# Branch B of a two-layer diffusion step: softmax sums from ScalarE's accumulator, and two passes with the values in place of three

## The reference, cut to what matters

```
s_band = einsum(qb, kband)            # |i - j| <= 128, else -1e30
s_ctx  = einsum(qb, k_ctx)            # 128 cached context keys
s_sink = broadcast(sink)              # one logit per head
p = softmax(concat([s_band, s_ctx, s_sink]))
o = einsum(p_band, vband) + einsum(p_ctx, v_ctx)      # the sink's p is dropped
```

## Time and profile before

| | |
|---|---|
| runs | 1607.69, 1608.44 (median), 1612.07 us |
| the profiled execution's own time | 1607.28 us, span 1605.5 us |
| TensorE (matmul) | 1458.1 us busy, 91% |
| VectorE | 833.1 us, 52% |
| GpSimd | 781.1 us, 49% |
| ScalarE | 550.6 us, 34% |
| mean granted TensorE clock | 0.968 |
| branch B attention | about 376 to 521 us (layer 0) and 1175 to 1320 us (layer 1) |

### The profile page before, as it was taken

The page is one execution under the profiler, slowest core; times in us unless marked ns, Lnnn a source line. Parts: engine busy times, 40 slices in busy tenths (PEclk is TensorE's granted clock), DMA queues, the critical chain, the costliest instruction groups (busy, mean ns, idle before and its releaser), DMA issues.

```text
span 1605.5 us, 21685 instructions
## 1 busy us (share of the span) xinstructions
PE 1458.1 (91%) x8776; PEld 1316.6 (82%) x8776; DVE 833.1 (52%) x1257; ACT 550.6 (34%) x821; POOL 781.1 (49%) x542
## 2 busy tenths in 40 slices
PE   4998998999998999899919999989999989998995
PEld 3798888899887888898718888887998879998984
DVE  4675677453788411103665676764438774011056
ACT  3233554234642211223122245542345432221221
POOL 1444675324675434645342456762246754464453
PEclk9999999999999999999969999999999999999998
DMA  7312000212010444253113220002121012214311
GB/s 306 131 53 70 27 27 16 87 59 66 27 41 27 146 145 169 79 183 120 40 31 114 70 67 26 27 28 80 55 66 35 32 56 102 79 66 171 107 64 66
DMA packets 36612, 126.90 MB, mean 79 GB/s; under 512 B 5024, under 2 KB 5664, under 8 KB 36512
## 3 DMA queue, kind: packets, MB, share of 16 engines
q1 hardware_dynamic: 29808, 108.54, 19.9%
q10 hardware_dynamic: 6704, 16.97, 2.9%
HBM read 119.73 MB, written 5.77 MB: 78 GB/s over the span
## 4 chain that ended last, share of the span: by engine, by line
PE 79%; DVE 10%; POOL 4%; issue 2%; ACT 2%; DMA 0%; POOLq 0%; DVEq 0%; ACTq 0%
PE ps L833 41%; PE ps L785 6%; PE ps L787 6%; PE ps L786 6%; PE ps L928 2%; PE ps L930 2%; PE ps L980 2%; PE ps L957 2%; PE ps L977 2%; DVE o_inv L1494 2%; PE ps L956 2%; PE ps L978 2%; POOL w_lo L1589 1%; PE ps L850 1%; DVE x L1546 1%
## 5 line engine op out<-in xcount | busy, mean ns | idle before, releaser
L1589 POOL TENSOR_TENSOR w_lo<-raw,w_hi 128x1024 fp32r<-128x1024 f32 x150 | 363.4, 2430 | 353.6 <-ACT w_hi L1026 353.2
L833 PE MATMUL ps<-h_hi,w_hi 128*128 128x320 f32 x1280 | 299.3, 315 | 13.6 <-DVE g_c L1506 6.4
L833 PE MATMUL ps<-h_lo,w_hi 128*128 128x320 f32 x1280 | 293.6, 311 | 0.0
L833 PE MATMUL ps<-h_hi,w_lo 128*128 128x320 f32 x1280 | 293.0, 310 | 0.0
L1609 POOL TENSOR_TENSOR p_lo<-p_f,p_hi 128x512 fp32r<-128x512 f32 x164 | 212.8, 1301 | 154.9 <-ACT p_hi L1137 154.7
L833 PEld LDWEIGHTS ps<-h_hi,w_hi 128*128 128x128 f32 x1280 | 218.2, 189 | 34.5 <-issue 8.7
L833 PEld LDWEIGHTS ps<-h_lo,w_hi 128*128 128x128 f32 x1280 | 217.1, 190 | 2.5
L833 PEld LDWEIGHTS ps<-h_hi,w_lo 128*128 128x128 f32 x1280 | 216.1, 189 | 2.4
L1026 ACT ACTIVATE w_hi<-raw 128x1024 fp32r<-128x1024 f32 x150 | 154.8, 1050 | 99.2 <-DMA raw<-in_weights 44.4
L1521 DVE TENSOR_TENSOR gy<-ps,sg 128x640 f32<-128x640 f32 x32 | 26.4, 824 | 255.7 <-PE ps L833 255.6
L1444 DVE TENSOR_REDUCE top<-ps 128x1 f32<-128x512 f32 (+1 forms) x128 | 83.5, 657 | 120.7 <-PE ps L935 87.0
(11 more groups left out here) (164 smaller groups left out, 2589.7 us busy)
## 6 DMA issues: line engine op xcount, KB each, us to landing
raw<-in_weights SPq DMA_DIRECT2D x190, 512.0 KB, 3.3
raw_more<-in_weights SPq DMA_DIRECT2D x10, 512.0 KB, 10.8
x<-in_x_sample ACTq DMA_DIRECT2D x6, 512.0 KB, 8.2
x_mid<-x ACTq DMA_DIRECT2D x5, 512.0 KB, 4.4
x<-x_mid ACTq DMA_DIRECT2D x5, 512.0 KB, 6.5
y_sample<-x SPq DMA_DIRECT2D x4, 512.0 KB, 2.7
pack<-in_pack ACTq DMA_DIRECT2D x2, 528.0 KB, 4.7
x<-in_x_sample SPq DMA_DIRECT2D x2, 512.0 KB, 5.0
```

The lines of the kernel that those rows point to most:

```text
L833: last = pe.matmul(ps[:, s + half, 0:HALF], w[:, u % RING, cols], acts[:, k, half * HALF:(half + 1) * HALF], start=k == 0 and part == 0, s ...
L1589: did(pool.tensor_tensor(w_lo[:, n % RING, :], raw_tile(r), w_hi[:, n % RING, :], ALU.subtract), w_ready)
```

## The change

In branch B alone:

- `S` no longer serves only the maximum. VectorE takes the maximum and makes minus max(top, sink) in one more small instruction (`neg_made`); then ScalarE takes the exponential of the same scores in place in PSUM, with that as its bias and with `accum_out` into `sums`. The bank is drained by ScalarE now. In tile 0 these are four exponentials of 128 columns.
- `dg`, the sink's step, its `p_hi`, `p_lo`, its two passes and the ones tile are gone: 30 steps per layer remain. 
- New, `su` on VectorE: sums + exp(sink - max), reciprocal, and a split in hi and lo, four instructions of 128x4. New, `it`: a transpose of the 128x8 on TensorE, and VectorE spreads it over `inv_m` (8 x 512). New, `iv`: one matmul of 512 columns with `first_rows` (ones in 8 rows), whose result ScalarE copies to `inv_b` (64x512).
- `PV` has two passes: the stationary tile is [v_lo, v_hi] by `p_hi`, then [v_hi, 0] (or [0, v_hi] for the other head) by `p_lo`. So O comes in two halves of the rows. `O` on VectorE is, for odd and even heads each, a copy of one half (64x256 from PSUM), the addition of the other and the multiplication by the inverse. The bank is drained after the second addition.
- Order: `tick()`, which puts out the `O`, `og`, `oh`, `ol`, `iv` events that are due, comes before `ST` in both branches. In branch B, `it` stands before the `ST` three steps after the group's first, and `S`, `row`, `es`, `su` come after the step's `PV`. The filler is spread over 30 steps instead of 40.
- Banks: in branch B, `row`, `it` and `iv` take banks 2 and 3 in turn with `ST`; `S` has 0 and 1 for itself.
- `zeros` (GpSimd, small memset) and `neg_sink`, `two_by_four`, `first_rows` (small constants) are new.

```diff
@@ attention()
         if br == "b":
             early[max(first[g] - row_ahead, -1)].append(("es", l, br, g))
+            early[first[g]].append(("su", l, br, g))
...
         if i == len(group_slots(br, g)) - 1:
-            later.append([1, ("O", l, br, g, 0)])
-            later.append([2, ("O", l, br, g, 1)])
+            if br == "a":
+                later.append([1, ("O", l, br, g, 0)])
+                later.append([2, ("O", l, br, g, 1)])
+            else:
+                later.append([1, ("iv", l, br, g)])
+                later.append([2, ("O", l, br, g, 1)])
...
+    def turn_inverse(n):
+        if br == "b" and n >= 0 and steps[n][1] == 0:
+            out.append(("it", l, br, steps[n][0]))
+
     for n, (g, i) in enumerate(steps):
-        if group_slots(br, g)[i] == SINK:
-            out.append(("dg", l, br, g))
+        tick()
+        turn_inverse(n - lag)
         out.append(("ST", l, br, g, i))
-        out.extend(early[n])
-        tick()
+        if br == "a":
+            out.extend(early[n])
         if n >= lag:
             product(n - lag)
+        if br == "b":
+            out.extend(early[n])
         fill()
     for n in range(len(steps) - lag, len(steps)):
         tick()
+        turn_inverse(n)
         product(n)
@@ bank_plan()
-        elif kind in ("S", "row"):
+        elif kind in ("S", "row") and e[2] == "a":
             take(e, 1, turn["S"] % 2)
             turn["S"] += 1
...
+        elif kind in ("row", "it", "iv", "ST"):
             take(e, 1, 2 + turn["ST"] % 2)
             turn["ST"] += 1
@@ TensorE
+                    elif kind == "it":
+                        s = begin(e)
+                        pe.wait_ge(inv_made, NO[e] + 1)
+                        did(pe.transpose(ps[0:2 * GRP, s, 0:P], inv_r[:, NO[e] % 3, :].bitcast(F32), ident), filled[s])
+                    elif kind == "iv":
+                        s = begin(e)
+                        wait_drained(pe, ("it",) + e[1:])
+                        did(pe.matmul(ps[:, s, :], first_rows[:, :], inv_m[:, :], start=True, stop=True), filled[s])
...
+                            both, high = v_pair(slot_key, kv)
+                            pe.matmul(ps[:, b, :], both, p_hi[:, n % 3, :], start=i == 0, stop=False)
                         pe.wait_ge(p_lo_made, n + 1)
                         last = pe.matmul(ps[:, b, :], high, p_lo[:, n % 3, :], start=False, stop=ends)
@@ ScalarE
+                    elif kind == "S" and e[2] == "b":
+                        _, l, br, g, i = e
+                        c = NO[("row",) + e[1:4]] % 3
+                        s = wait_filled(act, e)
+                        act.wait_ge(neg_made, NEG_NO[e] + 1)
...
+                        for h, cols in runs:
+                            last = act.activation(ps[:, s, cols], ps[:, s, cols], ACT.Exp, bias=top_r[:, c, h:h + 1].bitcast(F32),
+                                                  accum_out=sums[:, c, h:h + 1])
+                        did(last, drained[s])
+                    elif kind == "iv":
+                        s = wait_filled(act, e)
+                        if NO[e]:
+                            act.wait_ge(inv_used, NO[e])
+                        did(act.activation(inv_b[0:HD, :], ps[0:HD, s, :], ACT.Copy), drained[s])
@@ VectorE
+                            after(did(dve.tensor_reduce(top[:, c, 0, mine], src, axis=AX.X, op=ALU.max)))
+                            sinks = slice(kv * GRP + mine.start, kv * GRP + mine.stop)
+                            did(dve.scalar_tensor_tensor(top_r[:, c, mine], top[:, c, 0, mine], -1.0, neg_sink[:, sinks], ALU.mult,
+                                                         ALU.min), neg_made)
...
-                        for h in range(GRP):
-                            last = dve.tensor_scalar(p_f[:, n % 3, h * P:(h + 1) * P], ident, es_f[:, c, h:h + 1], None, ALU.mult)
-                            did(last, dg_made if h == GRP - 1 else None)
+                        after(did(dve.tensor_tensor(inv_f[:, n % 3, :], sums[:, c, :], es_f[:, NO[("es",) + e[1:]] % 3, :], ALU.add)))
+                        after(did(dve.reciprocal(inv_f[:, n % 3, :], inv_f[:, n % 3, :])))
+                        after(did(dve.tensor_scalar(inv_r[:, n % 3, 0:GRP], inv_f[:, n % 3, :], 1.0, None, ALU.mult)))
+                        did(dve.tensor_tensor(inv_r[:, n % 3, GRP:2 * GRP], inv_f[:, n % 3, :], inv_r[:, n % 3, 0:GRP], ALU.subtract),
+                            inv_made)
...
+                        if br == "b":
+                            for odd in range(2):
+                                dst = og_sum(n)[head_rows(odd), :, :]
+                                parts = [by_head(ps[o_rows(i), b, :])[:, odd:GRP:2, :] for i in range(2)]
+                                inv = by_head(inv_b[0:HD, :])[:, odd:GRP:2, :]
+                                after(did(dve.tensor_copy(dst, parts[1])))
+                                added = dve.tensor_tensor(dst, parts[0], dst, ALU.add)
+                                if odd:
+                                    drain(added, stage)
+                                else:
+                                    after(did(added))
+                                    wait_drained(dve, ("iv",) + e[1:4])
+                                did(dve.tensor_tensor(dst, inv, dst, ALU.mult), inv_used if odd else None)
+                            continue
```

More of the change, by code:

```diff
@@ L26 @@
 GROUPS = [(kv, t) for t in (1, 2, 3, 4, 0) for kv in range(NKV)]
+FIRST_GROUP = {t: min(g for g, group in enumerate(GROUPS) if group[1] == t) for t in range(T)}
 KT_D = D // P
@@ L53, in key_slots @@
 def key_slots(br, tile):
-    last = [(SINK, None)] if br == "b" else []
     if tile == 0:
-        return [(0, None)] + last
+        return [(0, None)]
     if br == "a":
@@ L110, in attention @@
             early[max(first[g] - row_ahead, -1)].append(("es", l, br, g))
+            early[first[g]].append(("su", l, br, g))
         start = end
     for n in early:
-        early[n].sort(key=lambda e: (e[0] == "S", e[3]) if n >= 0 else (e[3], e[0] != "S"))
+        turn = ("row", "es", "su", "S")
+        early[n].sort(key=lambda e: (e[0] == "S", e[3], turn.index(e[0])) if n >= 0 else (e[3], e[0] != "S"))
     filler = list(filler)
@@ L239, in layer_order @@
     out.append(("pool", 0, 1, 2, 3, 4, 5, 6, 7))
+    out.append(("zeros", l))
     out.extend(mm("kv_b"))
@@ L453, in bank_plan @@
             take(e, 1)
-        elif kind in ("S", "row"):
+        elif kind in ("S", "row") and e[2] == "a":
             take(e, 1, turn["S"] % 2)
             turn["S"] += 1
-        elif kind == "ST" and group_slots(*e[2:4])[e[4]] != SINK:
+        elif kind == "ST" and e[2] == "a":
+            take(e, 1, 2 + turn["ST"] % 2)
+            turn["ST"] += 1
+        elif kind == "S":
+            take(e, 1, turn["S"] % 2)
+            turn["S"] += 1
+        elif kind in ("row", "it", "iv", "ST"):
             take(e, 1, 2 + turn["ST"] % 2)
@@ L529 @@
 ROWS = [e for e in ORDER if e[0] == "row"]
-O_STAGES = [e[:4] for e in ORDER if e[0] == "O" and e[4] == 0]
+O_STAGES = [e[:4] for e in ORDER if e[0] == "O" and e[4] == 1]
+TOP_NO = {e: n for n, e in enumerate(e for e in ORDER if e[0] == "row" and e[2] == "a")}
+NEG_NO = {e: n for n, e in enumerate(e for e in ORDER if e[0] == "S" and e[2] == "b")}
+TURNED_INV = [e for e in ORDER if e[0] == "iv"]
 O_PER_LAYER = sum(e[0] in ("ol", "mix") for e in ORDER) // DEPTH
@@ L971, in _ @@
                         pe.wait_ge(p_hi_made, n + 1)
-                        if slot_key == SINK:
-                            high = one_row[:, kv:kv + 2, :].rearrange("p s d -> p (s d)")
-                            pe.matmul(ps[:, b, :], high, p_hi[:, n % 3, :], start=False, stop=False)
-                        else:
+                        if br == "a":
                             high, low = v_blocks(slot_key, kv)
@@ L1327, in _ @@
                             dve.wait_ge(rope_loaded, 16)
+                            after(did(dve.tensor_tensor(two_by_four[0:2 * GRP, :], setup[0:2 * GRP, 0, 0:GRP],
+                                                        setup[0:2 * GRP, 0, GRP:2 * GRP], ALU.add)))
+                        did(dve.tensor_scalar(neg_sink[:, :], sink, -1.0, None, ALU.mult))
                         after(did(dve.tensor_scalar(norm[:, 1, :, :], norm[:, 1, :, :], float(HD) ** 0.5, None, ALU.mult)))
@@ L1464, in _ @@
                             before = ROWS[n - 3]
-                            last = max(i for i, key in enumerate(group_slots(*before[2:])) if key != SINK)
-                            wait_filled(dve, ("ST",) + before[1:] + (last,))
+                            wait_filled(dve, ("ST",) + before[1:] + (len(group_slots(*before[2:])) - 1,))
                         did(dve.tensor_copy(by_head(q_m[0:HD, n % 3, :]), q_t[0:HD, heads, tokens]))
@@ L1595, in _ @@
                         did(pool.memset(vv[:, :, 1, 1, :].bitcast(F32), 0.0), ones_ready)
```

(3 more changed lines are left out.)

124 lines of the change are left out of this document (81 added, 43 removed).

## The result

The changed kernel takes **1659.94 us** (median of four, 1655.65 to 1666.32) against 1608.75 us before: a ratio of 1.0318, 95% interval 1.0280 to 1.0355. It is slower by 51 us, where 1598 us, faster, was forecast. The profiled execution took 1666.32 us (span 1664.5), 6 us above the median.

What follows compares the result with a forecast made beforehand. TensorE's instruction stream was taken as the bound. The terms -16.2 + 18.2 - 13.4 + 1.0 = -10.4 us against the profiled 1607.28 gave 1596.9, forecast as a 1598 us median; range 1579 to 1614, about 1 in 10 outside either side.

Steps and rivals of the forecast that it cites:

- Work, -16.2: TensorE in branch B: 50 matmuls fewer, 10 `iv` and 10 `it` more per layer, -16.2 us for both layers.
- The wait of `ST`, +18.2: Branch B: `ST` waits for ScalarE's copy of `iv` to free its bank, 14 times 1.3 us, +18.2 us.
- rival C: A draw: `ST` waits of 1.7 us (+24) and a tail as long as before; 1604 to 1612 us, chance 0.18.
- the 8.8 + 3.0 = 11.8 us of before become 5.1: Branch B: TensorE's holes (8.8 us) and slow clock behind them (3.0) shrink to 5.1 us a layer, -13.4 in all.
- ScalarE's +1.0: Branch B under Silu: small `g_c` waits stay, 0.5 us a layer added for ScalarE being behind, +1.0 us (0 to 8).
- Its tail: End of branch B: serial `iv`, copy, `O`, `it` leave 3.1 us of holes, the longest 2.5 before `iv` 9.
- VectorE, 99 us forecast: VectorE's busy time in branch B's stretch goes from 110 to about 99 us a layer, or 89 to 114.
- The exponential with an accumulator: ScalarE, branch B: a score exponential of 512 columns with accumulator should read 0.6 to 0.8 us.
- ScalarE's sum: ScalarE's busy time in branch B's stretch goes from 70 to 94 us of some 140, not the bound.
- Branch A's order, 0: Branch A: the new `tick` order costs nothing, since the scores are four steps ahead.
- Rival B: Slower: ScalarE's queue holds TensorE from `iv` to `ST` (+42), other ScalarE waits +8, holes -12; 1630 us, chance 0.18.
- wrong altogether if ScalarE's queue makes TensorE wait in the `S` banks too: Branch B sign of failure: TensorE waits in `S` banks, or the 145 us stretch doesn't shrink about 5 us per layer.

Runs made afterwards that it cites:

- e8: Changed kernel without score exponentials, `su`, `it`, `iv`, the copy and the multiplication by the inverse; output not normalised: 1585.60 us, 0.9856 of the kernel before.
- e4: Changed kernel without ScalarE's score exponentials; sums a constant, banks drained by VectorE's maximum: 1624.41 us, 1.0090 of the kernel before.
- e3: Changed kernel with each score exponential one step later in ScalarE's order, `iv` left in place: 1644.65 us, 1.0213 of the kernel before.
- e9: Changed kernel with branch A's due events behind `ST` again, as in the kernel before: 1660.36 us, 1.0321 of the kernel before.
- e1: Kernel before with one edit: in branch A alone, due events stand ahead of `ST`: 1613.05 us, ratio 1.0031.
- e5: Changed kernel with `iv` behind the step's `PV`, `it` behind its `S`, and score exponentials one step later on ScalarE: 1642.29 us, 1.0213 of before.
- e10: Changed kernel with score exponentials kept, but without `su`, `it`, `iv` and the multiplication by the inverse; output not normalised: 1601.41 us, 0.9949 of before.
- e11: Kernel before with the sink's step replaced by its exponential turned, spread and added to the sums by one matmul per group; three value passes: 1636.20 us, 1.0168.

## Why the prediction was wrong, step by step

- **Work, -16.2.** Right: counted matmul by matmul it is -16.5, and e8's 100 passes are -23.4. The balance's -10.6 has 5.3 us of holes in it.
- **The wait of `ST`, +18.2.** Right in place and number, and mis-sized: 14 of 1.77 us, +24.8, which is rival C's figure (1.7). The term took a score exponential in front of the copy that is 0 to 0.4 us late, and a `w_hi` in one group of four; the traces show `p_hi`, exponential, read and `w_hi` in a row, or an exponential that has itself waited up to 1.4 us for VectorE. Without the exponentials (e4) the wait is 0.74 us, the forecast's 0.83.
- **The failed step is "the 8.8 + 3.0 = 11.8 us of before become 5.1", -13.4 us.** It supposed that TensorE's other waits shrink since "no piece now blocks as long". They grew by 16.8 us, and the clock's loss by 18.3 us: the term and ScalarE's +1.0, forecast as -12.4 together, measured +35.1. Its tail was the right size in all (forecast 3.1 us of holes, measured 1.31 + 1.59) but not in its place: the holes stand before `iv` 8 and `PV` 9, and the hole of 2.5 us before `iv` 9 is not there. L1506's waits of 3.2 us shrank to one of 2.1, and were to be gone; what was missed lies in the steps ahead of the tail. There 19 of 40 score exponentials hold ScalarE's queue for VectorE's `neg` (26.4 us of waits a layer; e4 and e3 show what they cost), and VectorE has `su`'s four dependent instructions and a spread more per group. I priced busy time, and looked for lateness only in front of the copy.
- **VectorE, 99 us forecast, 110.45 measured** (382 to 551 us, the window with the same tail). The small instructions were at the upper end of the range: `neg` and `su` sum to (35.6 + 4.5)/2 + (9.9 + 9.7 + 9.4 + 3.6)/2 = 36.3 us a layer (4.5 for the four `neg` of four columns and 3.6 for the reciprocals, rows not shown), 22 taken of 12 to 37.
- **The exponential with an accumulator**, forecast 0.6 to 0.8 us for 512 columns: right. Its rows read 0.655 and 0.195 for the read, but they overlap. From start to start the exponential takes 0.585 (median of 32) and the read 0.093 when something is queued behind it: 0.68 us, and 0.57 and 0.34 for 384 and 128 columns. That is 22.7 us a layer where 23.7 were forecast, and ScalarE's sum was right, 94.86 for 94. The price nobody had seen was not the trouble.
- **ScalarE under Silu, +1.0.** `g_c` waits went from 1.0 us a layer to 5.6 and 4.7: +8 over both. ScalarE was busy only 28.14 of 40 us there, not 35: it stood still for 12 of the 40 us, so being full is not what makes it late.
- **Branch A's order, 0.** The medians of e9 agree; e1 says 4 us in the kernel before, and the traces some 2 us a layer in branch A, the cover of four steps notwithstanding.

Rival B had the sign and the engine: ScalarE's in-order queue at `iv` to `ST`. But its deciding point was a wait above 2.0 us, and the waits stayed below, at 1.77; the kernel was slower all the same, because of the waits it had at +8 and -12, and of the clock. The sentence "wrong altogether if ScalarE's queue makes TensorE wait in the `S` banks too" came true: 2.2 us a layer after, 7.5 in e5. So did its other half: branch B's stretch didn't shrink by 5 us a layer, it grew by 23.2 and 26.2.

That the clock's 18.3 us follow from the holes is read from the traces, not tested apart: no run changed the clock alone. In e8 and e10, whose holes are few (7.5 and 13.9 us of waits in layer 0), its loss in branch B is 2.9 and 3.1 us over both layers. How much of the 18.3 us a given hole brings stays open: e10 has 3 us more of waits a layer than before and no more loss to the clock (3.1 against 3.4 us), and e11's two layers, with the same 686 matmuls and 14.9 and 15.1 us of waits in the branch, take 145.9 and 139.9 us, at a mean granted clock of 0.93 and 0.98.

## What to carry to other kernels

A bound engine's saved passes are worth their price only if what replaces them does not put new links between in-order queues: price the latency from one engine to the next and what stands in each queue behind a wait, not the busy time, which for ScalarE was forecast rightly here and said nothing. Leave a wide margin for the clock behind added holes of TensorE: here 18.3 us came with 41.6 us of added waits, and in e10 none with 6. And test the saving first with the replacement left out (e8), then put the pieces back one by one; two pieces that each look bearable (15.8 and 38.8 us) can cost a third more together. Where two orders of the same events are compared, read the stage's length in the traces: a difference of 2 us was there in every one of them, and in the medians it came out as 4, 0 and 13.

## What the runs showed of the hardware

- `accum_out` brings a second instruction on ScalarE each time, whatever the width. Its row reads 189 ns at least, median 193, 216 at most, in 80; but it starts 75 to 85 ns before the exponential's row ends, and what is queued behind it starts a median of 93 ns after it. So it costs about a tenth of a microsecond. The row of an exponential of 512 columns in PSUM with a bias is 655 ns, that of a plain one 597.
- Most of VectorE's smallest instructions have a median of a sixth of a microsecond, and some a long tail. After, whole span (min/median/max in ns):

```profile
L1513 DVE SCALAR_TENSOR_TENSOR top_r<-top,neg_sink x68: 158/160/2086, 384.3 to 1345.5; 128x1 fp32r<-128x1 f32 x64, 128x4 fp32r<-128x4 f32 x4
L1556 DVE TENSOR_TENSOR inv_f<-sums,es_f x20: 140/162/1147, 406.7 to 1360.5; 128x4 f32<-128x4 f32 x20
L1557 DVE RECIPROCAL inv_f<-inv_f x20: 177/178/179, 406.9 to 1361.2; 128x4 f32<-128x4 f32 x20
L1558 DVE TENSOR_SCALAR inv_r<-inv_f x20: 169/310/1120, 407.1 to 1361.4; 128x4 fp32r<-128x4 f32 x20
L1586 DVE COPY o_sum<-ps x40: 425/427/429, 435.9 to 1373.2; 64x256 f32<-64x256 f32 x40
L1593 DVE TENSOR_TENSOR o_sum<-mod_row,o_sum x40: 416/422/1058, 436.8 to 1374.1; 64x256 f32<-64x256 f32 x40
```

The lines with two SBUF operands reach 1 to 2 us, the reciprocal and the copy out of PSUM never vary; in the timeline above, L1559 took 2.27 us while GpSimd's `w_lo` of 2.37 us ran. This is the rule of the Trainium skill, SBUF — State Buffer, section "Who interferes with whom": two SBUF inputs on VectorE contend with a GpSimd instruction that reads SBUF. The trace agrees: of the 108 instructions of L1513, L1556 and L1559, 42 were stretched, and each of these ran beside a GpSimd instruction and ended with it. It adds that the mean (556 ns for one column) is what a chain of such instructions costs, 3.5 times the median. And L1558, with one operand in SBUF, was stretched as well, ten times in twenty and in the same way, which the rule of two inputs doesn't cover. The prediction weighed this at +4 us and left it out of its sum.
- A hole of TensorE doesn't decide alone whether the clock falls: in layer 0 after, holes of 2.48, 2.17 and 2.88 us were followed by the lower level, those of 2.30, 2.10 and 2.06 us were not, and 1.91 and 1.59 us ones, with other holes close before them, were. Nor does the stream around it: in layer 1, with the same 658 matmuls, the holes in the places of the 2.30 and the 2.06 (2.29 and 2.05 us) were followed by the lower level.
